# Two-layer hybrid trunk with experts: gated features turned by VectorE in 32x32 squares, down weights loaded in pieces of 8 KB

## What is computed

```python
def swiglu(h, w1, w3, w2):
    return (jax.nn.silu(h @ w1) * (h @ w3)) @ w2

def moe_swiglu(h, w_router, w1, w3, w2):
    logits = jnp.einsum('bsd,de->bse', h, w_router).astype(jnp.float32)
    top_val, top_idx = lax.top_k(logits, TOP_K)
    top_w = jax.nn.softmax(top_val, axis=-1)
    gates = jnp.sum(jax.nn.one_hot(top_idx, N_EXPERTS, dtype=jnp.float32) * top_w[..., None], axis=-2)
    out = jnp.zeros_like(h)
    for e in range(N_EXPERTS):
        out = out + gates[..., e:e + 1].astype(h.dtype) * swiglu(h, w1[e], w3[e], w2[e])
    return out
```

## Time and profile before

| | |
|---|---|
| median of 3 runs | 1421.65 us |
| lowest, highest | 1421.26, 1421.77 us |
| the profiled execution: time | 1422.79 us |
| the profiled execution: span on the page | 1421.0 us |
| TensorE busy | 1382.7 us, 97% |
| VectorE, ScalarE busy | 348.2 us, 277.6 us |
| experts (first up block to end of last down) | 495.5 to 1404.8 us |
| moved by DMA | 431.36 MB, mean 304 GB/s |

### The profile page before, as it was taken

How to read it: one execution, slowest core, us unless ns; L and a number is a source line. 1 busy time by engine, 2 the same in 40 slices (tenths; PEclk the granted TensorE clock), 3 DMA queues, 4 the chain that set the end, 5 groups by cost and what they waited for, 6 DMA issues and landing times.

```text
span 1421.0 us, 32940 instructions
## 1 busy us (share of the span) xinstructions
PE 1382.7 (97%) x14890; PEld 808.2 (57%) x14890; DVE 348.2 (25%) x428; ACT 277.6 (20%) x353; POOL 21.1 (1%) x36
## 2 busy tenths in 40 slices
PE   6999899999999999999999999999999999999995
PEld 4998788888998833534543443453453353454343
DVE  4568544435566510010010001001001001001001
ACT  4554433323662300000000000001001000000001
POOL 1000000000000000000000000000000000000000
PEclk9999999999999999999999999999999999999998
DMA  7834655513735499999999999999999999999960
GB/s 231 303 120 141 216 195 196 189 56 120 275 119 224 176 355 385 397 385 378 402 388 387 394 390 375 401 391 384 396 385 392 385 394 381 386 399 393 376 251 32
DMA packets 140354, 431.36 MB, mean 304 GB/s; under 512 B 12346, under 2 KB 18778, under 8 KB 140096
## 3 DMA queue, kind: packets, MB, share of 16 engines
q1 hardware_dynamic: 138672, 424.01, 78.8%
q0 software_dynamic: 1552, 5.32, 1.1%
HBM read 427.19 MB, written 2.10 MB: 302 GB/s over the span
## 4 chain that ended last, share of the span: by engine, by line
PE 95%; DVE 2%; DMA 1%; ACT 1%; issue 1%; SPq 0%; POOL 0%; DVEq 0%; POOLq 0%; ACTq 0%
PE psum L1638 41%; PE psum L1665 20%; PE psum L1224 8%; PE psum L1226 8%; PE psum L1225 8%; PE psum L1648 2%; PE psum L1396 1%; DMA raw<-in_w_mix_in 1%; PE psum L1680 1%; DVE wlo L805 0%; DVE h L818 0%; PE psum L1611 0%; PE psum L1612 0%; ACT whi L565 0%; DVE x L977 0%
## 5 line engine op out<-in xcount | busy, mean ns | idle before, releaser
L1638 PE MATMUL psum<-ring,xe 128*32 128x512 f32 (+1 forms) x5952 | 568.9, 538 | 0.0
L1638 PEld LDWEIGHTS psum<-ring,xe 128*32 128x32 f32 x5952 | 189.5, 110 | 343.7 <-issue 308.6
L1665 PE MATMUL psum<-ring,gT 128*32 128x256 f32 x5376 | 296.0, 379 | 0.6 <-ACT gT L738 0.6
L1665 PEld LDWEIGHTS psum<-ring,gT 128*32 128x32 f32 x5376 | 174.6, 110 | 125.8 <-issue 13.8
L1120 DVE TENSOR_TENSOR gate<-gate,psum 128x768 f32<-128x768 f32 (+1 forms) x32 | 27.3, 854 | 601.3 <-ACT gate L733 601.3
L805 DVE TENSOR_TENSOR wlo<-raw,whi 128x2048 fp32r<-128x2048 f32 (+1 forms) x67 | 147.4, 2229 | 53.9 <-ACT whi L565 53.9
L565 ACT CAST whi<-raw 128x2048 fp32r<-128x2048 f32 (+1 forms) x67 | 122.3, 1860 | 60.9 <-PE psum L1226 32.5
L1224 PE MATMUL psum<-whi,f_hi 128*128 128x512 f32 (+1 forms) x320 | 125.7, 393 | 5.5 <-DVE wlo L805 4.7
L1226 PE MATMUL psum<-whi,f_lo 128*128 128x512 f32 (+1 forms) x320 | 123.5, 386 | 0.0
L1225 PE MATMUL psum<-wlo,f_hi 128*128 128x512 f32 (+1 forms) x320 | 123.1, 385 | 0.0
L738 ACT COPY gT<-psum 128x768 f32<-128x768 f32 (+1 forms) x32 | 23.0, 720 | 453.7 <-PE psum L1648 453.7
(11 more groups left out here) (210 smaller groups left out, 855.0 us busy)
## 6 DMA issues: line engine op xcount, KB each, us to landing
ring<-in_moe_w SPq DMA_DIRECT2D x672, 512.0 KB, 5.9
raw<-in_ffn_w SPq DMA_DIRECT2D x33, 1024.0 KB, 5.5
raw<-in_w_mix_in SPq DMA_DIRECT2D x22, 1024.0 KB, 7.4
raw<-in_w_mix_out SPq DMA_DIRECT2D x8, 1024.0 KB, 5.0
raw<-in_w_mix_in SPq DMA_DIRECT2D x4, 544.0 KB, 5.4
x<-in_x SPq DMA_DIRECT2D x2, 512.0 KB, 5.0
bias_by_distance<-setup_bias POOLq DMA_DIRECT2D x1, 1024.0 KB, 5.1
bias<-bias_by_distance POOLq DMA_DIRECT2D x2, 512.0 KB, 7.3
```

The source lines that it names most:

```text
L1638: ins = mm(banks(j)[o:o + 32, g, 0:2 * q].rearrange("p (i c) -> p i c", i=2), rows_[:, k * CAP + 32 * g:k * CAP + 32 * (g + 1)], w[:, kk, ...
L1665: ins = mm(bank[6 + g // 2][32 * q:32 * (q + 1), 256 * (g % 2):256 * (g % 2 + 1)], gT[:, a:a + 32], w[:, o:o + 256], start=j == 0 and n == ...
```

## The change

**Turning.** `e_turn` on TensorE and ScalarE's copy `turned` are gone, with the semaphore `e_gT_ps`. VectorE, right behind each product, waits for its own product and then writes `gT` with its transpose instruction, which turns each square of 32x32 by itself: one instruction over all three groups in steps 0 to 2, three in step 3. It reads `gate` in steps of two elements (`c` outer of `k`). `gT` has two buffers, one for even and one for odd steps; one of them takes the place of a part of `h`.

**Which feature lies where.** Turned square by square, partition 32 t + c of `gT` holds a feature of tile t. For these to be two neighbours in a row of the weights, the up columns are dealt to the tiles in runs of 64: tile t takes columns 64 t to 64 t + 63 of each 256. Loads of up weights are as they were; the matmul reads its moving operand in runs of 64. The two squares that come from one run (even and odd columns) give partition p of `gT` the features 256 n + 2 p and 256 n + 2 p + 1.

**Down loads.** A down slot then holds rows 256 n + 2 p and 256 n + 2 p + 1 of `w2` in partition p, which is 8 KB in a row in HBM. The slot is still filled by two DMAs of 512 KB; the first now covers partitions 0 to 63, the second 64 to 127, with 8 KB for each partition.

**Order.** TensorE's list has the up blocks of a step in one piece; the rest of its order is as before.

```diff
--- before.py
+++ after.py
@@ -233,7 +233,8 @@
         gate_at = at[0]
         gate = [place(f"gate{i}", GROUPS * 256) for i in range(2)]
         pick = [place(f"pick{i}", NT * 4 * CAP, F32R, offset=gate_at + i * 4 * NT * 4 * CAP) for i in range(2)]
-        gT = place("gT", GROUPS * 256)
+        gT = [place(f"gT{i}", GROUPS * 256, offset=o) for i, o in enumerate((at[0], h_at + 4 * GROUPS * 256))]
+        at[0] += 4 * GROUPS * 256
         y_hi = place("y_hi", GROUPS * 256, F32R)
         y_lo = place("y_lo", GROUPS * 256, F32R, offset=h_at)
         pickT = place("pickT", GROUPS * SEQ, F32R)
...
@@ -426,12 +427,12 @@
 
             def load_down(f, e, turn, j):
 
-                w = moe_w2[0].rearrange("e (k p) c -> p e k c", p=P)
-                for b in range(4 if j < STEPS - 1 else 2):
+                w = moe_w2[0].rearrange("e (n p k) d -> n p e (k d)", p=P, k=2)
+                for b in range(QUARTER[j] // 64):
                     to, until = free_slot(f + b, turn)
-                    for i in range(2):
-                        k = 8 * j + 2 * b + i
-                        sp.dma_start(to[:, D * i:D * (i + 1)], w[:, ds(turn + e, 1), k, :].rearrange("p e c -> p (e c)")
+                    for i in range(0, P, 64):
+                        src = w[4 * j + b, i:i + 64, ds(turn + e, 1), :].rearrange("p e x -> p (e x)")
+                        sp.dma_start(to[i:i + 64, :], src
                                      ).wait_op(moe_used, until, "sem-ge").then_inc(moe_full[(f + b) % RING], 16)
 
             def expert(sweep, e, turn=0, last=False):
@@ -732,15 +733,9 @@
                 q = QUARTER[j]
                 nc.scalar.activation(by_group(gate[j % 2][:], q), banks(j)[:, :, 0:q], ACT.Silu).then_inc(e_silu, 1)
 
-            def turned(sweep, j, e, turn):
-                act.wait_ge(e_gT_ps, STEPS * turn + (STEPS * (EXPERTS * sweep + e) + j + 1))
-                q = QUARTER[j]
-                nc.scalar.copy(by_group(gT[:], q), banks(j)[:, :, 0:q]).then_inc(e_gT, 1)
-
             def expert(sweep, e, turn=0, last=False):
                 for j, p in enumerate((-1, 7, 19, 27)):
                     silu(sweep, j, p, e, turn)
-                    turned(sweep, j, e, turn)
                 act.wait_ge(moe_used, blocks_done(sweep, PER_EXPERT * e + (33 if last else 37), turn))
                 nc.scalar.copy(y_hi[:], psum[:, 6 * 512:6 * 512 + GROUPS * 256]).then_inc(y_sb, 1)
 
@@ -1118,6 +1113,12 @@
                 q = QUARTER[j]
                 hidden_ = by_group(gate[j % 2][:], q)
                 nc.vector.tensor_tensor(hidden_, hidden_, banks(j)[:, :, q:2 * q], ALU.mult).then_inc(e_g, 1)
+                dve.wait_ge(e_g, STEPS * turn + (STEPS * (EXPERTS * sweep + e) + j + 1))
+                for o, n in ((0, GROUPS * q),) if j < STEPS - 1 else tuple((256 * g, q) for g in range(GROUPS)):
+                    a = o * q // 256
+                    ins = nc.vector.transpose(gT[j % 2][:, a:a + n].rearrange("p (b k s) -> p b k s", k=2, s=32),
+                                              gate[j % 2][:, o:o + n].rearrange("p (b c k) -> p b k c", c=32, k=2))
+                ins.then_inc(e_gT, 1)
 
             def picks_turned(e, turn):
                 if isinstance(turn, int):
@@ -1635,36 +1636,28 @@
                         for g in range(GROUPS):
                             for t in range(4):
                                 o = 32 * t
-                                ins = mm(banks(j)[o:o + 32, g, 0:2 * q].rearrange("p (i c) -> p i c", i=2),
+                                ins = mm(banks(j)[o:o + 32, g, 0:2 * q].rearrange("p (i b c) -> p i b c", i=2, c=64),
                                          rows_[:, k * CAP + 32 * g:k * CAP + 32 * (g + 1)],
-                                         w[:, kk, :, q * t:q * (t + 1)], start=k == 0, stop=k == KD - 1)
+                                         w[:, kk, :, :].rearrange("p i (b t c) -> p i b t c", t=4, c=64)[:, :, :, t, :],
+                                         start=k == 0, stop=k == KD - 1)
                     ins.then_inc(moe_used, 1)
 
-            def e_turn(sweep, j, e, turn):
-
-                pe.wait_ge(e_g, STEPS * turn + (STEPS * (EXPERTS * sweep + e) + j + 1))
-                for g in range(GROUPS):
-                    for b in range(QUARTER[j] // P):
-                        ins = pe.transpose(banks(j)[:, g, b * P:(b + 1) * P],
-                                           gate[j % 2][:, 256 * g + b * P:256 * g + (b + 1) * P], ident())
-                ins.then_inc(e_gT_ps, 1)
-
             def e_down(sweep, j, f, e, turn):
 
                 pe.wait_ge(e_gT, STEPS * turn + (STEPS * (EXPERTS * sweep + e) + j + 1))
-                nb = QUARTER[j] // P
-                for n in range(4 * nb):
-                    t, b = n // nb, n % nb
+                q_ = QUARTER[j]
+                tiles = q_ // 32
+                for n in range(tiles):
                     w = ring[(f + n // 2) % RING]
                     if n % 2 == 0:
                         arrived(f + n // 2, turn)
                     for g in range(GROUPS):
-                        a = 256 * g + b * P + 32 * t
+                        a = q_ * g + 32 * n
                         for q in range(4):
                             o = 1024 * (n % 2) + 256 * q
                             ins = mm(bank[6 + g // 2][32 * q:32 * (q + 1), 256 * (g % 2):256 * (g % 2 + 1)],
-                                     gT[:, a:a + 32], w[:, o:o + 256], start=j == 0 and n == 0 and g != 1,
-                                     stop=j == STEPS - 1 and n == 4 * nb - 1, skip_group_check=True)
+                                     gT[j % 2][:, a:a + 32], w[:, o:o + 256], start=j == 0 and n == 0 and g != 1,
+                                     stop=j == STEPS - 1 and n == tiles - 1, skip_group_check=True)
                     if n % 2:
                         ins.then_inc(moe_used, 1)
 
@@ -1686,19 +1679,12 @@
                 v = turn + (EXPERTS * sweep + e)
                 f = PER_SWEEP * sweep + 8 + PER_EXPERT * e
                 pe.wait_ge(added, v + 1)
-                e_up(1, f, turn, xe, range(0, 4))
-                e_turn(sweep, 0, e, turn)
-                e_up(1, f, turn, xe, range(4, 8))
+                e_up(1, f, turn, xe, range(0, 8))
                 e_down(sweep, 0, f + 8, e, turn)
-                e_up(2, f + 12, turn, xe, range(0, 4))
-                e_turn(sweep, 1, e, turn)
-                e_up(2, f + 12, turn, xe, range(4, 8))
+                e_up(2, f + 12, turn, xe, range(0, 8))
                 e_down(sweep, 1, f + 20, e, turn)
-                e_up(3, f + 24, turn, xe, range(0, 2))
-                e_turn(sweep, 2, e, turn)
-                e_up(3, f + 24, turn, xe, range(2, 4))
+                e_up(3, f + 24, turn, xe, range(0, 4))
                 e_down(sweep, 2, f + 28, e, turn)
-                e_turn(sweep, 3, e, turn)
                 if last:
                     e_down(sweep, 3, f + 32, e, turn)
                     scatter(v)
```

More of the change, by code:

```diff
@@ L300, in trunk @@
         moe_full = [sem(f"moe_full{i}") for i in range(RING)]
-        moe_used, e_silu, e_g, e_gT_ps, e_gT = (sem(n) for n in ("moe_used", "e_silu", "e_g", "e_gT_ps", "e_gT"))
+        moe_used, e_silu, e_g, e_gT = (sem(n) for n in ("moe_used", "e_silu", "e_g", "e_gT"))
         pick_sb, xe_ps, xe_act, xe_dve, xe_sb, pickT_sb = (
```

## The result

The changed kernel takes 1785.09 us (median of four runs, 1771.31 to 1792.41) against 1421.45 us before: a ratio of 1.2548, interval 1.2465 to 1.2631. It is slower by a quarter. The forecast was 1395.8 us, the end of the stated range 1600, and the rival that named this cause (B, the loads into half of the partitions) had 1627 us as its full price. So two things have to be explained: the direction, and 158 us that the rival hadn't counted.

A forecast was written before the change was run, and what follows sets the result against it. TensorE was taken as the bound, at 113.62 us an expert; 3.17 us off each of eight (25.4) plus 0.55 in the last make 25.9, so 1421.65 - 25.9 = 1395.75 us, range 1391 to 1600.

The forecast's parts named there:

- B: Experts' down blocks: half-partition loads at 205 GB/s become the bound, 1627 us at full price, 1590 likeliest; chance 0.32.
- Transposes leave TensorE: TensorE's chain in the experts: 3.17 us less for each of eight, 0.55 more in the last, 25.9 us in all.
- VectorE turns the squares: VectorE behind each product: a large transpose takes 0.9 us, at most 3.8, hidden behind TensorE's work; cost nothing.
- Runs of 64: Up matmuls' moving operand in eight runs of 64 columns: taken as zero cost, from above 7 us in all.
- Down loads: Ring loads for down blocks: today's rate kept, 410 GB/s against 399 needed, so loads stay ahead; from above, 205 GB/s.
- Its term for the half blocks: Ring loads of the 112 remaining down blocks: 5.11 us each at 205 GB/s, in place of 2.56.
- Its term for the up blocks: Ring loads of the 210 remaining up blocks: unchanged at 2.56 us each.
- Its threshold: Down-block loads: seen only under 345 GB/s (3.04 us a block); kernel slower than before under 320 GB/s (3.28 us).
- the price is partial: Half-partition down loads: if DMA engines are apart in time, some on each half, 270 GB/s gives 1489 us.
- an SP queue that waits no more: Sign that half-partition loads are the bound: the loading queue no longer waits for matmuls to free ring slots.
- C: Loads in the experts: engines sustain only 392 GB/s, an expert takes 112.3 us, gain 10 us, 1411 us; chance 0.09.
- D: Down matmuls still wait for gT; in the loop this needs a transpose of over 18.9 us; given no chance.

## Why the prediction was wrong

**What bounds the kernel before: right.** It is TensorE, with loads that have some margin. (The 375 to 402 GB/s "in every slice of the experts" leave out their first slice, which has 355.)

**Transposes leave TensorE: right to a tenth.** 25.9 us were forecast. The three kernels with all of the change but the partition halves are at 1396.1 to 1397.4 us, where 1395.8 were forecast, and 26.2 to 27.5 us under the kernel before in the same set of runs. A middle step of the new expert takes 20.60 + 10.36 us, as built.

**VectorE turns the squares: right.** The large ones take 0.98 us and the small ones 0.27; 0.9 and about 0.3 were taken. The three times that the down waited in the changed kernel, 7.0 us with the weight loads, don't occur in the kernel split by columns.

**Runs of 64: right.** They cost nothing that is seen.

**Down loads: this is the step that failed.** "I take today's rate: the trace shows DMA engines at a steady rate on the same bytes, and nothing in it that ties the rate to partitions." The trace couldn't show it, as it has no large load into half of the partitions, and silence was taken for evidence. The bound from above that stood in the same paragraph, 205 GB/s, was near the truth: the packets of the half loads make 221. The Trainium skill's "SBUF — State Buffer" had it: 196 GB/s for 64 partitions (section "Door 1: The DMA port swizzle") and 6% more for two such DMAs at once (section "Can I just issue two DMAs to hit both halves?"). The runs lie near that, with 221 GB/s in a queue that is seldom idle. With one unknown that had a factor of two between its ends and a margin of 3 us in 110 on it, a chance of 0.32 for the dear end was too low, I think.

**The rival's own sum was mis-sized.** Its term for the half blocks, 112 x 5.11 = 572 us, measures 531 (112 x 4.74), and with 531 its sum gives 1586 us, next to the 1590 that it called likeliest. The kernel took 199 us more than that (158 more than the full price of 1627). Its term for the up blocks, 210 x 2.56 = 537 us, is where the size went wrong: an up load is not free of the halves. That term was held at the rate of a queue whose engines keep step; in the changed kernel they don't. Its threshold was wrong for the same reason. It said that loads in halves are seen under 345 GB/s in all 14 blocks; 2 of 14 at 221 cost 44 us, where the same sum gives none. That the half pairs might drift apart was weighed only as a relief ("the price is partial"), and the runs have it beside the surcharge. Two of its signs failed with this: TensorE waited longer for loads in the up blocks (433.7 us) than in the down blocks (225.9), and the median landing was 18.0 us, not over 30. The sign of "an SP queue that waits no more" failed too: it waited 270.9 us behind L1639.

**C and D: no part in it.** In the kernel split by columns the engines sustain 401 to 402 GB/s with the loader waiting, so the margin is there, and the down never waits for gT.

## What to carry to other kernels

Split a transfer by columns, or by every other partition, and not into partitions 0 to 63 and 64 to 127, even where both halves are in flight one behind the other: here each half ran at about half the rate, so that the two together took 1.9 times as long. When DMA is within a few per cent of the compute that it feeds, an untested shape of load is the main term of the forecast, whatever the edit was meant for. And a load is complete when its slowest engine is: a queue that is far ahead of its user hides that one engine of sixteen is late only until the lead is used up.

## What the runs showed of the hardware

- A float32 load of 512 KB into partitions 0 to 63 or 64 to 127 has packets of 8 KB at 593 ns in the changed kernel, 1.9 times the 317 ns of one into all, or into every other partition; packets of 4 KB into all partitions take 165 to 168 ns.
- Packets of 4 KB into all partitions take 288 ns where they begin beside two or more half packets, and 173 beside none (changed kernel, 600 to 1300 us).
- A stream of 512 KB loads over 128 partitions sustains 401 GB/s beside TensorE at work, with stretches of 408. This is what TensorE asked; down loads of 1 MB give the same time.
- When half loads and full loads alternate in a long queue, the last two of a slot's 32 arrivals come 16 and 18 us after the first, the thirtieth after 4.8; I read this as one of sixteen DMA engines that is late. Emptying the queue 31 times (3.5 us each) won 63 us.
- The transpose of VectorE on 128x768 float32, read in steps of two elements, takes 0.98 us beside 0.95 for the product of the same size.
